# Ten conditions repeated in the moving operand of the modulation tiles, and six single tiles of each layer moved from the spatial stage into the projections

## The reference, cut to what matters

```python
def run_group(x, c, ssm0, conv0, W):
    for l in range(DEPTH):
        mod = jax.nn.silu(c) @ W['w_mod'][l] + W['b_mod'][l]
        sh1, sc1, g1, sh2, sc2, g2 = [t[:, None, :] for t in jnp.split(mod, 6, axis=-1)]
        h = rmsnorm(x, W['mix_pre_g'][l]) * (1 + sc1) + sh1
        ...
        merged = jax.nn.sigmoid(ga) * (ya @ W['w_ssd_out'][l]) + jax.nn.sigmoid(gb) * (yb @ W['w_cmlp_out'][l])
        x = x + g1 * rmsnorm(merged @ W['w_o'][l], W['mix_post_g'][l])
        h = rmsnorm(x, W['ffn_pre_g'][l]) * (1 + sc2) + sh2
        ...
        x = x + g2 * rmsnorm(f, W['ffn_post_g'][l])
```

## Time and profile before

| what | value |
|---|---|
| runs (us) | 2011.82, 2017.2, 2029.72; median 2017.2 |
| the profiled execution | 2018.74 us, of which the span from first to last instruction is 2017.0 us |
| PE busy | 1932.5 us (96%) |
| DVE / ACT busy | 1346.4 us (67%) / 1005.2 us (50%) |
| mean granted TensorE clock over the span | 0.929 |
| HBM read | 452.84 MB |

### The profile page before, as it was taken

How to read it: one execution, slowest core, us unless ns; L and a number is a source line. 1 busy time by engine, 2 the same in 40 slices (tenths; PEclk the granted TensorE clock), 3 DMA queues, 4 the chain that set the end, 5 groups by cost and what they waited for, 6 DMA issues and landing times.

```text
span 2017.0 us, 34497 instructions
## 1 busy us (share of the span) xinstructions
PE 1932.5 (96%) x13768; PEld 1845.8 (92%) x13768; DVE 1346.4 (67%) x1654; ACT 1005.2 (50%) x983; POOL 63.7 (3%) x95
## 2 busy tenths in 40 slices
PE   8899999999999999999999599999999999999995
PEld 8899899999999999989999598989999999999994
DVE  0457746644444545774653688887888788888885
ACT  0254624322333325471422366766676677667772
POOL 4000100000000000010000000000000000000000
PEclk9899979887999979996978699999999999999998
DMA  8255753564665725576353399998999899999990
GB/s 244 68 171 182 232 187 106 177 188 133 199 191 183 213 84 168 179 231 187 107 176 95 110 348 347 348 342 284 347 344 349 286 353 338 357 301 362 335 352 22
DMA packets 421111, 465.29 MB, mean 231 GB/s; under 512 B 11044, under 2 KB 393204, under 8 KB 420979
## 3 DMA queue, kind: packets, MB, share of 16 engines
q1 hardware_dynamic: 413970, 441.65, 68.2%
q0 software_dynamic: 6720, 20.86, 3.3%
q10 hardware_dynamic: 304, 1.08, 0.2%
HBM read 452.84 MB, written 10.92 MB: 230 GB/s over the span
## 4 chain that ended last, share of the span: by engine, by line
PE 87%; DVE 7%; ACT 3%; issue 2%; DMA 1%; POOL 0%; DVEq 0%; ACTq 0%; SPq 0%; POOLq 0%
PE acc L767 11%; PE acc L367 9%; PE acc L368 9%; PE acc L374 8%; PE acc L1121 8%; PE acc L1125 8%; PE acc L1122 8%; PE acc L1154 4%; PE acc L1160 4%; PE acc L1155 4%; PE ms L716 2%; ACT whi L307 1%; PE ms L1079 1%; PE ms L1103 1%; DVE wlo L312 1%
## 5 line engine op out<-in xcount | busy, mean ns | idle before, releaser
L332 DVE TENSOR_TENSOR wlo<-raw,whi 128x2048 fp32r<-128x2048 f32 x220 | 503.8, 2292 | 90.2 <-ACT whi L327 89.5
L327 ACT ACTIVATE whi<-raw 128x2048 fp32r<-128x2048 f32 x220 | 420.9, 1914 | 79.1 <-PE acc L1160 73.7
L367 PE MATMUL acc<-xhi,whi 128*128 128x264 f32 x1584 | 423.9, 301 | 7.6 <-DVE xlo L1516 5.5
L368 PE MATMUL acc<-xlo,whi 128*128 128x264 f32 x1584 | 417.0, 298 | 0.0
L312 DVE TENSOR_TENSOR wlo<-raw,whi 128x2048 fp32r<-128x2048 f32 x112 | 256.7, 2292 | 235.4 <-ACT whi L307 234.7
L1121 PE MATMUL acc<-whi,hghi 128*128 128x256 f32 x1408 | 351.7, 287 | 3.6 <-issue 2.0
L1122 PE MATMUL acc<-whi,hglo 128*128 128x256 f32 x1408 | 345.3, 282 | 4.2 <-issue 4.2
L367 PEld LDWEIGHTS acc<-xhi,whi 128*128 128x128 f32 x1584 | 319.9, 202 | 14.2 <-issue 11.3
L368 PEld LDWEIGHTS acc<-xlo,whi 128*128 128x128 f32 x1584 | 320.3, 202 | 0.1
L1122 PEld LDWEIGHTS acc<-whi,hglo 128*128 128x128 f32 x1408 | 267.1, 190 | 4.8 <-issue 4.6
L1121 PEld LDWEIGHTS acc<-whi,hghi 128*128 128x128 f32 x1408 | 266.3, 189 | 4.9 <-issue 4.7
(11 more groups left out here) (362 smaller groups left out, 2263.7 us busy)
## 6 DMA issues: line engine op xcount, KB each, us to landing
raw<-in_exp_wd_dram SPq DMA_DIRECT2D x76, 1024.0 KB, 5.8
raw<-in_exp_wg_dram SPq DMA_DIRECT2D x72, 1024.0 KB, 6.8
raw<-in_exp_wu_dram SPq DMA_DIRECT2D x72, 1024.0 KB, 7.4
raw<-in_w_in_dram SPq DMA_DIRECT2D x52, 1024.0 KB, 5.3
xraw<-in_w_mod_dram SPq DMA_DIRECT2D x46, 512.0 KB, 4.6
late<-in_w_mod_dram SPq DMA_DIRECT2D x34, 512.0 KB, 6.7
hf<-in_exp_wu_dram SPq DMA_DIRECT2D x16, 1024.0 KB, 7.1
hf<-in_exp_wg_dram SPq DMA_DIRECT2D x16, 1024.0 KB, 6.7
```

Source lines behind the costliest of these rows:

```text
L327: act.activation(whi[j % R3], raw6[slot], ACT.Copy).then_inc(sem["hi_ready"], 1)
L332: dve.tensor_tensor(wlo[j % R3], raw6[slot], whi[j % R3].bitcast(F32), ALU.subtract) \
L367: pe.matmul(out, a, hi(k), start=first and k == 0, stop=False)
L368: pe.matmul(out, a, lo(k), start=False, stop=False)
```

## The change

Three things are done. `unit` repeats the ten columns up to twelve times through an access pattern with a step of zero, so that the moving operand has 120 columns (less for the last three of the first sixteen tiles, where the bank ends); only the first ten results are kept, and the next tile overwrites the rest. The six single tiles at `vs`, `diag`, `taken`, `mix0`, `y_taken` and `mix1` leave these places in both layers: three more stand at `ssd_mid` and three more at `w_o_mid`. `FEED` is adapted, and the wait for `merged` moves from a place of the queue to tile `U1`, the first that needs it.

```diff
-        FILL = ({"gb": 1, "vs": 1, "w_turned": 3, "diag": 1, "taken": 1, "mix0": 1, "y_taken": 1, "mix1": 1, "gate": 2,
-                 "ssd": 3, "ssd_mid": 1, "w_o": 2, "w_o_mid": 1, "norm2": 5, "norm3": 5, "g0": 2,
+        FILL = ({"gb": 1, "w_turned": 3, "gate": 2, "ssd": 3, "ssd_mid": 4, "w_o": 2, "w_o_mid": 4, "norm2": 5, "norm3": 5, "g0": 2,
                  **{f"g{i}": 1 for i in range(1, FP)}, "end": 2, "norm4": 5},
-                {"norm1": 5, "gb": 1, "vs": 1, "w_turned": 4, "diag": 1, "taken": 1, "mix0": 1, "y_taken": 1, "mix1": 1,
-                 "gate": 2, "ssd": 4, "ssd_mid": 2, "w_o": 2, "w_o_mid": 3, "norm2": 3})
+                {"norm1": 5, "gb": 1, "w_turned": 4, "gate": 2, "ssd": 4, "ssd_mid": 5, "w_o": 2, "w_o_mid": 6,
+                 "norm2": 3})
...
+                    if u == U1:
+                        sp.wait_ge(sem["merged"], 2)
...
-                out = mod_sums(q, RIDERS[q].index(v))
+                at = RIDERS[q].index(v)
+                times = min(12, (512 - 272) // NC - at)
+                out = mod_sums(q, at, times).rearrange("p (r c) -> p r c", c=NC)
                 for k in range(KT):
-                    ins = pe.matmul(out, weights(k), cT[:, k, :], start=k == 0, stop=k == KT - 1)
+                    ins = pe.matmul(out, weights(k), bc(cT[:, k, :], 1, [P, times, NC]), start=k == 0, stop=k == KT - 1)
```

More of the change, by code:

```diff
@@ L544, in feed @@
                 fed = max(fed, to)
[L546 to L549, removed]
+            FEED = ({("ga", 3): 3, ("cmlp_out", 1): 4, ("cmlp_out", 2): 7, ("ssd_out", 2): 12, ("ssd_out", 3): 13,
+                     ("w_o", 0): 15, ("w_o", 1): 17, ("w_o", 2): 18, ("w_o", 3): 24},
+                    {("xbc", 1): 48, ("xbc", 2): 53, ("ga", 3): 56, ("cmlp_out", 1): 57, ("cmlp_out", 2): 61,
+                     ("ssd_out", 2): 67, ("ssd_out", 3): 69, ("w_o", 0): 71, ("w_o", 1): 73, ("w_o", 2): 74,
                      ("w_o", 3): 80})
@@ L557, in after @@
                             sp.wait_ge(sem["conv_done"], l + 1)
-                        if (name, c) == ("w_o", 2) and l == 0:
-                            sp.wait_ge(sem["merged"], 2)
                         feed(FEED[l][name, c])
```

## The result

The median of the runs is 1957.42 us (1953.87 to 1962.32), beside 2015.14 us (2011.82 to 2029.72) of the kernel before on the same chip: a ratio of 0.9702, 95% interval 0.9655 to 0.975. The forecast was 1957 us.

What follows compares the result with a forecast made beforehand. The prediction took PE, busy 96% of the span, as the bound, with modulation tiles at half clock. Its terms made -66.5 us, less 5 us kept for a falling clock: -61.5, giving 1957 us, range 1940 to 1988.

Steps and rivals of the forecast that it cites:

- The projections: Twelve single tiles added at `ssd_mid` and `w_o_mid`, with refill waits, less clock gains: +16 us.
- the 5 us kept in reserve: Allowance for the clock still falling at times where PE waits and transposes between tiles: 5 us.
- Width and clock: All wide tiles: 120 columns act like 128, raise PE's clock and lie under the weight load; forecast chance 0.74.
- The start: First tiles, transposes and norm sums, up to the first product: 33.4 us instead of 58.9, -25 us.
- Unmixed blocks: Rival: clock rises at start, norms and projections, not among transposes and short waits; 1981 us, chance 0.12.
- The 24 us: Gain forecast for tiles that stay in the spatial stage and ahead of `ssd_out`, from running at full clock: -24.
- Waits in the place of the clock: Rival: refills or loads cost more, 3 us instead of 0.5 at nine refills; 1979 us, chance 0.07.
- nothing kept at `g0`: Alternative condition of the waits rival: none of the 7.5 us at layer 0's norms survives the load wait; 1979 us.
- Spatial and state stages: Both layers up to `ssd_mid`: -24 for tiles that stay and -9 for tiles that leave, together -33 us.
- the -9: Six single tiles leaving PE's waits at `vs`, `diag`, `taken`, `mix0` and others: -4.5 us in each layer.
- Norms of layer 0: Two blocks of five tiles at full clock and a shorter sum, partly lost to a late load at `g0`: -9 us.
- Change of layer: The same -6 and -7.5 as at layer 0's norms, no load behind, and -2 at the first product: -15.5 us.

Runs made afterwards that it cites:

- width alone: The kernel before with tiles widened to 120 columns, every tile left at its old place; 1936.15 us, ratio 0.9595.

## Why the prediction was right, term by term

The mechanism was the forecast one, and the stages sum to -56.7 for -61.5. That the median meets 1957 us to 0.4 us is luck. The projections cost 8.8 us more than forecast, which the 5 us kept in reserve and 3.8 us of the expert stage, not forecast at all, happen to cover; and the profiled execution, the slowest of the four, is still 4.8 us short of the forecast gain.

**Width and clock: right.** This was the step on which the forecast rested, read from the spatial product's 128 columns. The start gave 24.7 us for 25, the five-tile blocks 9.09 us for 9.1, and the records at the start are 3.73 / 32 = 117 ns apart for 114. That the start ran at half clock before is read from its spacing alone, 214 ns, beside the 220 ns at a granted clock of 0.50 in the earlier trace rows; the clock column shows 1.00 there before and after. The kernel with 240 columns shows where the columns begin to be paid. Of the cause the runs show that the granted clock goes with the number of columns in these tiles: the second five of layer 0 take 13.98 us at 0.62 in the kernel with ten columns at the norms, and 9.09 us at 1.00 in after. Why it does, no run shows.

**Unmixed blocks: its price did not come.** The forecast gave 0.12 to a clock that stays low among transposes. Windows of before and after over the same stretch, the tiles of `w_turned` with the transposes around them, first before, then after (length, PE, weight loads, DVE, ACT, POOL, granted clock, DMA, GB/s):

```profile
271.90:291.40 19.50, 19.27 (x90) 19.14 (x90) 5.00 (x26) 2.21 (x3) 1.42 (x2) 0.50 0.63 188
```

```profile
243.60:253.50 9.90, 8.38 (x72) 7.99 (x72) 5.46 (x27) 1.98 (x3) 1.42 (x2) 1.00 1.11 329
```

The granted clock was 0.50 with tiles of ten columns and 1.00 with 120, with the same 24 transposes between (before has the tile of `diag` in the stretch as well). The 24 us that this rival takes away were not lost. Of transposes with no tiles between them this shows nothing: in this stretch tiles stand between the transposes.

**Waits in the place of the clock: in part.** The sum allowed about 0.5 us for a refill, and the rival 3 us at nine of them. Measured were 11.2 us in eight waits, and 6.49 us at `g0`. The rival's other condition, nothing kept at `g0`, is worth only the 3 us that the sum had kept, not 22.

**Where the clock did fall.** Windows of after at two tiles behind a wait for a load, `ssd_mid` and `g0` of layer 0:

```profile
355.00:358.00 3.00, 2.99 (x17) 3.00 (x18) 0.00 (x0) 0.00 (x0) 0.00 (x0) 0.64 1.19 306
...
445.50:452.10 6.60, 6.58 (x34) 6.60 (x35) 0.00 (x0) 0.00 (x0) 0.00 (x0) 0.55 1.16 293
```

PE is busy through both windows, with wide tiles, at clocks of 0.64 and 0.55. Ahead of them PE had stood 1.96 and 6.49 us. These waits are so paid a second time, with 1.0 us at the one and 2.9 at the other. It is not so behind every wait: the tile behind 3.21 us in layer 1 ran at a granted clock of 1.00, 2.04 us. And at layer 0's `ssd_mid` itself, in the kernel with ten columns at the norms, whose code up to there is the same, it did not happen (timeline of PE):

```profile
349.48 2.04 PE L770 MATMUL acc<-cT,xraw 128*128 128x120 f32 x16 [2.18 <-DMA xraw<-in_w_mod_dram]
```

The 5 us kept for a falling clock named this cause, waits of PE, but no place.

**Spatial and state stages: the sum nearly right, its split not.** -31.9 for -33. The single tiles' departure was priced at their length at half clock (3.4 us at `diag`, at a granted clock of 0.50). Once wide, such a tile takes 1.94 us and covers a wait of 1.2 to 2.2 us that comes back without it. Against width alone their departure brought 1.75 us in layer 0 and 3.0 in layer 1, 4.7 for the -9. In the state stage it brought nothing. Windows of layer 0 from the first transposes behind `taken` to the product behind `mix1`, first after, then width alone, which has three tiles more in it:

```profile
263.00:311.10 48.10, 44.36 (x326) 41.28 (x326) 31.77 (x52) 22.89 (x35) 0.00 (x0) 0.89 0.20 66
```

```profile
269.20:316.00 46.80, 46.41 (x374) 43.85 (x372) 31.91 (x54) 22.58 (x35) 0.00 (x0) 0.96 0.33 102
```

With the tiles gone PE waits more, its granted clock is 0.89 instead of 0.96, and the stretch is 1.3 us longer. What filled the gap was not forecast: the spatial product ran at a granted clock of 1.00 from its start, 7.2 us instead of 9.2 in each layer. Layer 1 gave less than was forecast for `w_turned`, for its third and fourth tile met loads. Timeline of PE of after at that place:

```profile
877.19 2.04 PE L770 MATMUL acc<-cT,xraw 128*128 128x120 f32 x16 [0.33 <-DMA xraw<-in_w_mod_dram]
882.02 3.77 PE L770 MATMUL acc<-cT,xraw 128*128 128x120 f32 x16 [2.79 <-DMA xraw<-in_w_mod_dram]
```

Here 0.5 us had been allowed; it was 3.12, and the tile behind ran at a granted clock of 0.50.

**Projections: the term that was mis-sized**, +24.8 for +16. The tiles themselves cost what was forecast. The refills were put at 2 us and waited 1.96 + 0.80 in layer 0 and 0.71 + 3.21 + 1.15 + 0.08 in layer 1, 7.9 us in all. Another 1.7 us went to the slow clock (0.64) behind the first of these waits: from that tile to `w_o` are 15.17 us in after and 13.49 in width alone, for the same tile and two products. The step that failed is the landing time of the refills. The sum took 4.1 us for each, from loads with no weight chunk beside them, and one refill for each place, where layer 1's five and six tiles need two and three. Those that PE waited longest for landed 5.5 and 7.7 us after their issue.

What made them late is shown only in part. The prediction named the weight chunks behind the loads and asked only when a chunk is wanted, not what it does to the tile's own load. At `ssd_mid` of both layers SP had waited at the tile's load with a chunk of 1 MB behind it, and issued the two 0.41 us apart; it did so at `w_o` of both layers as well. DMA issues of after in 349.4:350 and 984.6:985 (`ssd_mid` of layers 0 and 1), then 372.1:372.5 and 1007.9:1008.3 (`w_o`), with the time to landing at the end:

```profile
xraw<-in_w_mod_dram SPq DMA_DIRECT2D x1, 512.0 KB, 5.5
...
xraw<-in_w_mod_dram SPq DMA_DIRECT2D x1, 512.0 KB, 7.7
```

```profile
xraw<-in_w_mod_dram SPq DMA_DIRECT2D x1, 512.0 KB, 4.2
...
xraw<-in_w_mod_dram SPq DMA_DIRECT2D x1, 512.0 KB, 3.9
```

With a chunk right behind them the loads at `w_o` landed as fast as those of the earlier trace rows, so a chunk behind a load does not make it late by itself. The load of 7.7 us also left while the load of the tile before it had 2.4 us to go. In the kernel with the chunk ahead of the tile loads, the load at this place, again with another one under way, took 4.9 us, against 5.8 to 7.7 us in the four profiles with the order of after. For layer 1 that supports the chunk behind two loads in a row as the cause. For the 5.5 us of layer 0 the cause stays open: in the kernel with ten columns at the start the same load, with the same chunk 0.41 us behind it, landed in 4.0 us.

**Norms of layer 0**, -7.7 for -9. That a load would be late next at `g0` was right, and the kernel with its two tiles moved shows it: 9.5 us come back at that place. Of the 7.5 us (7.4 in the trace) 3 were to be kept, and 1.5 were, because the two tiles behind the wait ran at a granted clock of 0.55, 2.9 us more than the sum had for them.

**Change of layer**, -14.3 for -15.5: the sum between the tile blocks stayed at a granted clock of 0.54 here, 3.73 us where 2.0 was forecast.

## What to carry to other kernels

Where a few columns stand behind full weight loads, repeat them: up to 120 columns it cost next to nothing here, 117 ns a record at most for 114, and it raised the granted clock of the same stretch from 0.50 to 1.00; find out first, with more columns in the same kernel, where the columns begin to be paid. Leave small work in the waits that it fills, and price its removal at the speed that it will have after the change; moving it into stages where the engine has little wait cost 21 us of the 80. When PE gets faster, list the loads issued behind the faster stage: of the nine that PE waited for here each cost its wait, up to 6.49 us, and three a slow clock after it, 1.0 to 2.9 us more.

## What the runs showed of the hardware that was not expected

A column beyond those that are nearly free costs the f32 matmul 0.83 ns in a record (1.06 us between the pairs of 220 and 180 columns, 40 columns in each of 32 records). A load of 0.5 MB with a load of 1 MB issued 0.41 us behind it landed in 3.9, 4.2 and 5.5 us when no other load of SP was under way, and in 7.7 us when another tile's load was. Behind waits for loads of 1.96, 2.79 and 6.49 us PE ran the next tile or two at clocks of 0.64, 0.50 and 0.55, which made these waits cost 1.0 to 2.9 us more than themselves, but not behind one of 3.21 us in the same trace, nor behind one of 2.18 us at the place of the first in another kernel. What tells these apart stays open. The clock also fell in the middle of a product with PE busy throughout: in the kernel with tiles moved to `diag`, the window 280:283.3 has PE busy from end to end at 0.50. No run shows why.
